# Query weights as one transfer and page loads re-divided between GpSimd and SyncE in a hybrid decoder step

## What is computed

```python
h  = adaLN(rmsnorm(x)) @ w_in                 # 512 query, 6 x 128 key/value, gates, 1536 delta-net columns, ...
kc = compress_rows(cached and new cmp rows)   # silu(blocks of 32 rows @ w1) @ w2
o  = g0 * attend(q, kc, vc) + g1 * attend(q, selected blocks) + g2 * attend(q, window)   # 8 heads, 2 key/value heads
d  = gated_delta_rule(conv(qkv))
x  = x + gate1 * (w_out @ [o | d])
x  = x + gate2 * mixture_of_experts(adaLN(rmsnorm(x)))
```

## Time and profile before

| what | us |
|---|---|
| median of 3 runs (1308.56 to 1320.38) | 1310.61 |
| the profiled execution | 1313.39 |
| its span, first to last instruction | 1311.3 |
| TensorE busy | 1024.7 (78%) |
| VectorE, ScalarE, GpSimd busy | 459.6, 270.5, 254.5 |
| projection and page loads, up to the next stage's first work | 0 to 299.2 |
| attention | 631.4 to 784 |

### The profile page before, as it was taken

One profiled execution on the slowest core, in us unless ns is written; L12 is line 12 of the kernel. 1 busy time (PEld: TensorE's weight loads), 2 busy tenths in 40 slices (PEclk: granted clock), 3 DMA queues, 4 the chain that ended last, 5 costly groups with the idle time before them and its releaser, 6 DMA issues. The chain is left out here.

```text
span 1311.3 us, 22398 instructions
## 1 busy us (share of the span) xinstructions
PE 1024.7 (78%) x8897; PEld 688.6 (53%) x8897; DVE 459.6 (35%) x889; ACT 270.5 (21%) x598; POOL 254.5 (19%) x413
## 2 busy tenths in 40 slices
PE   4999999686999598978699778793197877977850
PEld 1547677464567487976456443442055554544430
DVE  2200000025452355665478440436121222312217
ACT  4100000005531200112467330100011111111114
POOL 5000361301010445020356320000300000000014
PEclk9899999797988798988599988896599888988975
DMA  9973699828000200000643108404799899999944
GB/s 344 357 261 135 199 269 251 195 62 290 33 6 1 33 3 3 3 2 6 163 98 106 51 10 274 193 0 192 227 322 384 338 382 366 379 383 362 384 146 163
DMA packets 94869, 241.83 MB, mean 184 GB/s; under 512 B 30653, under 2 KB 53749, under 8 KB 79079
## 3 DMA queue, kind: packets, MB, share of 16 engines
q1 hardware_dynamic: 75610, 183.39, 39.9%
q0 software_dynamic: 12928, 46.55, 12.7%
q10 hardware_dynamic: 6228, 10.44, 2.5%
HBM read 254.83 MB, written 49.21 MB: 232 GB/s over the span
## 5 line engine op out<-in xcount | busy, mean ns | idle before, releaser
L2293 PE MATMUL PS<-ring,mixT 128*64 128x256 f32 x448 | 117.9, 423 | 40.7 <-DMA ring<-in_expert_w_down_dram 36.2
L2294 PE MATMUL PS<-ring,mixT 128*64 128x256 f32 (+2 forms) x656 | 131.7, 356 | 1.3 <-DVE mixT L2390 1.3
L2293 PEld LDWEIGHTS PS<-ring,mixT 128*64 128x64 f32 x448 | 67.3, 154 | 84.5 <-issue 60.9
L515 PE MATMUL PS<-hT,wring 128*128 128x288 f32 x256 | 84.9, 414 | 11.9 <-DMA wring<-in_w_in_dram 11.9
L2404 DVE COPY heT<-PS 128x128 f32<-128x128 f32 x49 | 14.3, 292 | 213.0 <-PE PS L2312 213.0
L2294 PEld LDWEIGHTS PS<-ring,mixT 128*64 128x64 f32 x656 | 81.2, 149 | 7.1 <-issue 6.8
L516 PE MATMUL PS<-hT,wring 128*128 128x288 f32 x256 | 84.1, 411 | 0.0
L2068 PE MATMUL PS<-ring,mixT 128*128 128x512 f32 (+1 forms) x160 | 74.4, 627 | 9.2 <-DMA ring<-in_w_out_dram 9.2
L2328 PE MATMUL PS<-ring,heT 128*64 128x512 f32 (+2 forms) x164 | 62.0, 499 | 3.6 <-DVE heT L2404 3.6
L515 PEld LDWEIGHTS PS<-hT,wring 128*128 128x128 f32 x256 | 48.9, 193 | 29.2 <-DMA wring<-in_w_in_dram 12.3
L2279 PE MATMUL PS<-ident,mixT 64*128 64x64 f32 x392 | 35.6, 233 | 32.6 <-DMA mixT<-xs_dram 32.6
(11 more groups left out here) (483 smaller groups left out, 2075.8 us busy)
## 6 DMA issues: line engine op xcount, KB each, us to landing
ring<-in_expert_w_gate_dram SPq DMA_DIRECT2D x40, 1024.0 KB
ring<-in_expert_w_up_dram SPq DMA_DIRECT2D x40, 1024.0 KB
ring<-in_expert_w_down_dram SPq DMA_DIRECT2D x40, 1024.0 KB
raw<-in_w_ada_dram SPq DMA_DIRECT2D x8, 2048.0 KB
xs_dram<-mixT POOLq DMA_DIRECT2D x49, 256.0 KB, 24.5
mixT<-xs_dram POOLq DMA_DIRECT2D x49, 256.0 KB
ys_dram<-yr ACTq DMA_DIRECT2D x98, 128.0 KB
slot<-in_expert_w_gate_dram SPq DMA_DIRECT2D x9, 1024.0 KB
```

The costliest lines, as they stand in the source:

```text
L515: MM(PS[:, b, 0:HALF], lhs, hT[:, k, 0:HALF], **s)
L2293: MM(PS[R, b, 0:DE], xT[:, n % 2, q, :], wg[:, q, :], **s)
L2294: last = MM(PS[Q, b, lo:hi], xT[:, n % 2, q, :], wu[:, q, lo:hi], **s)
```

## The change

Four edits. The query weights come as one transfer like the other groups, and TensorE picks the two heads' 64 columns itself: each unit now has, per k and half of the tokens, two products of 64 columns, one into output partitions 0 to 63 and one into 64 to 127. GpSimd takes over the second half of the cmp_v pages in the front stage. In the middle stage TensorE turns the first pages before it waits for the position tables, and VectorE writes positions after them, with a new semaphore `xp_ok`. In attention SyncE loads all selected keys and the values of samples 0 and 1; GpSimd loads the values of samples 2 to 7, four pages ahead of each of its units 2 to 7, and keys and values have semaphores of their own.

```diff
@@ stage_front
-        slot_dmas[g % 3].append(KD * KV if g == QG else 1)
+        slot_dmas[g % 3].append(1)
...
-                if g == QG:
-                    for k in range(KD):
-                        for v in range(KV):
-                            sp.dma_start(wring[:, g % 3, k, 0:512].rearrange("p (g v d) -> p g v d", v=KV, g=G)[:, :, v],
-                                         wv[:, k, v * G * HD:(v + 1) * G * HD].rearrange("p (g d) -> p g d", g=G)).then_inc(w_in[g % 3], 16)
-                else:
-                    sp.dma_start(wring[:, g % 3, :, 0:w], wv[:, :, c:c + w]).then_inc(w_in[g % 3], 16)
+                sp.dma_start(wring[:, g % 3, :, 0:w], wv[:, :, c:c + w]).then_inc(w_in[g % 3], 16)
...
-            load_pages(nc, sp, NB // 2, NB, m, t["cache_cmp_v"], raw[1], m.raw_in[1])
             sp.wait_ge(b_out, 64)
...
             load_pages(nc, pool, 0, NB, m, t["cache_cmp_k"], raw[0], m.raw_in[0])
+            pool.wait_ge(b_ps, KD)
+            load_pages(nc, pool, NB // 2, NB, m, t["cache_cmp_v"], raw[1], m.raw_in[2])
...
-                    if chan:
+                    if g == QG:
+                        for hf in range(2):
+                            for v in range(KV):
+                                last = MM(PS[v * HD:(v + 1) * HD, b + hf, 0:HALF], wring[:, g % 3, k, (v * G + i) * HD:(v * G + i + 1) * HD],
+                                          hT[:, k, hf * HALF:(hf + 1) * HALF], **s)
+                    elif chan:
@@ stage_middle
+            def positions(s):
+                for v in range(KV):
+
+                    last = V.tensor_copy(xT[:, v, :, HCOL:], posT[:, s, :].rearrange("p (h r) -> p r h", r=OCT))
+                last.then_inc(xp_ok, 1)
...
+            take_pages(0)
             dve.wait_ge(pos_ps, 1)
             V.tensor_copy(posT[:, :, :], PS[:, 4, 0:2 * LP].rearrange("p (s l) -> p s l", s=2)).then_inc(pos_ok, 1)
             dve.wait_ge(pos_ok, 1)
-            take_pages(0)
+            positions(0)
...
+            turn_pages(0)
             pe.wait_ge(p_in, 16 * 2)
...
             last.then_inc(pos_ps, 1)
-            turn_pages(0)
...
             pe.wait_ge(tr_a, NU)
+            pe.wait_ge(xp_ok, 1)
@@ stage_attention
+    FIRST_LOAD = 2
...
+            def selected_keys(a):
+                load_pages(nc, sp, 2 * a, 2 * a + 2, m, t["cache_sel_k"], m.pages[:, SEL_K], selk_in[a])
...
-            selected(0)
+            selected_keys(0)
...
+            selected_keys(1)
             sp.dma_start(m.V[:, 1], window("cache_win_v")).then_inc(winv_in, 16)
...
-            for a in range(1, NB // 2):
-                selected(a)
+            load_pages(nc, sp, 0, 2, m, t["cache_sel_v"], m.V[:, 0], selv_in[0])
+            selected_keys(2)
+            selected_keys(3)
...
                 kind, br, a, g = units[u]
+                if FIRST_LOAD <= u < FIRST_LOAD + NB - 2:
+                    load_pages(nc, pool, u - FIRST_LOAD + 2, u - FIRST_LOAD + 3, m, t["cache_sel_v"], m.V[:, 0], selv_in[1])
...
-                        pe.wait_ge(*((sel_in[units[u][2]], 16 * 4 * PAGES) if br == SEL else (wink_in, 16)))
+                        pe.wait_ge(*((selk_in[units[u][2]], 16 * 2 * PAGES) if br == SEL else (wink_in, 16)))
...
                     if br == SEL and a == 0:
                         pe.wait_ge(new_in, 32)
+                        pe.wait_ge(selv_in[0], 16 * 2 * PAGES)
+                        pe.wait_ge(selv_in[1], 16 * (NB - 2) * PAGES)
```

More of the change, by code:

```diff
@@ L572, in stage_middle @@
     w_in, p_in, w2_in = [sem(f"c_w_in{s}") for s in range(2)], sem("c_p_in"), sem("c_w2_in")
+    xp_ok = sem("xp_ok")
     pos_ps, pos_ok, tr_ps, tr_a, tr_v = sem("pos_ps"), sem("pos_ok"), sem("tr_ps"), sem("tr_a"), sem("tr_v")
@@ L751, in taps @@
                         ins.then_inc(conv_ok, 1)
+            def positions(s):
+                for v in range(KV):
+                    last = V.tensor_copy(xT[:, v, :, HCOL:], posT[:, s, :].rearrange("p (h r) -> p r h", r=OCT))
+                last.then_inc(xp_ok, 1)
             def take_pages(s):
-                for v in range(KV):
-                    V.tensor_copy(xT[:, v, :, HCOL:], posT[:, s, :].rearrange("p (h r) -> p r h", r=OCT))
                 for n in range(NU):
@@ L772, in _ @@
             dve.wait_ge(hid_ps, KV * NHC)
+            positions(1)
             take_pages(1)
@@ L807, in turn_pages @@
                     if n == 1:
-                        pe.wait_ge(m.raw_in[s], 16 * NB * PAGES)
+                        pe.wait_ge(m.raw_in[s], 16 * (NB if s == 0 else NB // 2) * PAGES)
+                    if s == 1 and n == 1 + NB // 2:
+                        pe.wait_ge(m.raw_in[2], 16 * NB // 2 * PAGES)
                     for j in range(4):
@@ L889, in _ @@
             pe.wait_ge(tr_a, 2 * NU)
+            pe.wait_ge(xp_ok, 2)
             pe.wait_ge(w_in[1], 16)
@@ L1520, in stage_attention @@
     strip_in = [sem(f"a_strip_in{k}") for k in range(5)]
-    sel_in, wink_in, winv_in, new_in, bias_in = [sem(f"a_sel_in{a}") for a in range(NB // 2)], sem("a_wink_in"), sem("a_winv_in"), sem("a_new_in"), sem("a_bias_in")
+    selk_in, selv_in, wink_in, winv_in, new_in, bias_in = [sem(f"a_selk_in{a}") for a in range(NB // 2)], [sem(f"a_selv_in{k}") for k in range(2)], sem("a_wink_in"), sem("a_winv_in"), sem("a_new_in"), sem("a_bias_in")
     gate_out, gate_in, sg, qs_ok = sem("a_gate_out"), sem("a_gate_in"), sem("a_sg"), sem("a_qs_ok")
@@ L1600, in _ @@
                 sp.dma_start(strip[:, :, lo:hi], bass.AP(m.rb_rep, RB_C - (SEQ - P) + lo, [[H * RB_W - 1, P], [RB_W, H], [1, hi - lo]])).then_inc(strip_in[k], 16)
-            def selected(a):
-                load_pages(nc, sp, 2 * a, 2 * a + 2, m, t["cache_sel_k"], m.pages[:, SEL_K], sel_in[a])
-                load_pages(nc, sp, 2 * a, 2 * a + 2, m, t["cache_sel_v"], m.V[:, 0], sel_in[a])
+            def selected_keys(a):
+                load_pages(nc, sp, 2 * a, 2 * a + 2, m, t["cache_sel_k"], m.pages[:, SEL_K], selk_in[a])
             window = lambda name: t[name][0].rearrange("b (g p) k d -> p (b g) (k d)", p=P)
@@ L2532, in build @@
         m.rows_out = nc.alloc_semaphore("rows_out")
-        m.raw_in = [nc.alloc_semaphore(f"raw_in{s}") for s in range(2)]
+        m.raw_in = [nc.alloc_semaphore(f"raw_in{s}") for s in range(3)]
         m.ident = sb("ident", [P, P])
```

## The result

The changed kernel takes 1319.05 us (median of 20 runs, 1312.65 to 1325.78) where the kernel before takes 1310.78 beside it (20 runs). The ratio is 1.0062, interval 1.0043 to 1.0082: 8 us slower, within the 1% that was forecast, and not 1 us faster as the forecast's sum had it.

The account below looks back on a forecast made before the run. TensorE, busy 78%, was held by three 11 to 13 us waits: query weights, position tables (hiding a late barrier), samples' pages. Front -11.0, attention +23.5 and -13.7 sum to -1.2 us: forecast 1311, range 1298 to 1328.

Parts of the forecast that it names:

- Query group: End of the first stage: weights land in time, products take 31 us, TensorE ends at about 275.8 instead of 289.7.
- halves one after the other: Rival in the query group: paired 64-column products run serially, TensorE ends at 306.8, total 1328 us; chance 4%.
- GpSimd's last page: First stage: GpSimd, now with 48 pages, issues its last at 289.8, including 1 us delay from larger query weight transfers.
- Plus 1.4 for the barrier = 291.2.: First stage's end: only a 1.4 us barrier follows GpSimd's last page, so the middle stage starts turning pages at 291.2.
- The front and middle: First and middle stages together: 11.0 us saved, bounds -14 to -6.
- GpSimd ends no earlier than SyncE did: Rival in the front: slow page price for all 48 pages, last out at 303, front +2, total 1325; chance 6%.
- Attention, the cost: Units 2 to 7: GpSimd's four-page batches delay gate products, about 5.5 us a unit; +23.5 us, bounds +18 to +30.
- Attention, the gain: Samples' part of attention: TensorE's page waits and the half clock after them go; -13.7 us, bounds -12 and -15.
- The rule on VectorE and GpSimd's transfers: Attention: busy VectorE locks GpSimd out while writing descriptors; 24 loads could cost up to 60 us.
- The rival of dear pages: Attention: every GpSimd page costs 2.2 us, a batch 9.1 instead of 5.5, +21.6, total 1333; chance 12%.
- GpSimd hides its pages.: Rival in attention: loads fall into GpSimd's idle time, total 1288, half hidden 1300; chance 12% for 1300 or below.
- The sum: Whole kernel: -11.0 + 23.5 - 13.7 = -1.2 us, forecast time 1311.

Follow-up runs that it names:

- e7: Changed kernel with the query weights' last group in sixteen strided transfers and full-width products again; ratio 1.0051 to the kernel before (+6.7 us).
- e2: Changed kernel with attention's loads as before: SyncE loads keys and values of each pair, GpSimd none; ratio 0.9985 to the kernel before (-2.0 us).
- e3: Changed kernel with GpSimd's 24 attention value pages given to SyncE, keys still ahead of values; ratio 0.9871 to the kernel before (-16.9 us).
- e9: Changed kernel with GpSimd's 24 attention pages loaded one ahead of each of units 2 to 25, without the loop; ratio 0.9918 to the kernel before (-10.7 us).
- e5: Changed kernel with GpSimd also waiting for its last pages' arrival before the first stage ends; ratio 1.0069 to the kernel before (+9.0 us).
- e10: Changed kernel with the staging buffers' zero fills in 18 transfers instead of 66, same bytes; ratio 1.0047 to the kernel before (+6.2 us).

## Why the prediction came out as it did

The time was forecast as 1311 and is 1319; "within 1%" and the range hold, the sign of the sum (-1.2) does not. The attention part came out as worked out. The front part did not: 9 of its 11 us never came, and that the time still lies within 1% is the width of the band, not the merit of that part. By its steps:

**Query group.** Right. TensorE had the weights in time, took 31.26 us for the 128 products (256 passes) and ended at 275.7 (275.8). The rival of halves one after the other is out.

**SyncE's pages.** Right: its 16 pages take 21.99 and are out at 260.7 (265).

**GpSimd's last page.** Right: 289.85 (289.8). The 1 us for larger weight transfers among the zeros fits e7, where the last page is out 1.4 earlier, but is not shown by it: in six profiles with the same first stage the drain begins between 289.2 and 290.9.

**"Plus 1.4 for the barrier = 291.2."** This term failed. It was read from SyncE's end to the next stage, where the barrier is all that is left. Behind GpSimd's last page a drain of 9.62 and 1.1 of barrier follow. The kernel before had the drain of 8.52 in the same place, with nothing behind it; the change took its cover away. The first page turn came at 300.73 and not at 291.2, beyond the 297 that had been named as a sign of being wrong. The front and middle gave 2.0 by e2's time and 0.1 to 0.9 by the profiles (end of the middle stage 427.1 in the changed kernel and 426.3 in e2, 427.2 before) instead of 11.0, below the bound of 6: no bound had been set on GpSimd's way to the barrier. The 0.6 for the position copies can't be told from how much the middle stage varies between profiles. The rival "GpSimd ends no earlier than SyncE did" named this outcome with the wrong cause: the page price was the fast one, 1.28.

**Attention, the cost.** Right: +23.5 forecast, 25.0 measured by e3. A batch took 5.57 (5.5), six from unit 1 to 7 took 34.2 (33.0), units 8 to 10 gave 1.6 back (1.3). For the low clock behind the stretch 3 was forecast: from unit 10 to unit 27 the changed kernel takes 44.3 us and e3 41.4, with the clock at 0.50 up to 680 and 0.81 from 680 to 690, so 2.9. The drain at attention's end is longer by 2.0 for 24 more transfers. Its row, in the kernel before and in the changed one:

```profile
L1570 POOLq DRAIN  x1: 1154/1154/1154, 776.9 to 776.9; - x1
```

```profile
L1581 POOLq DRAIN  x1: 3147/3147/3147, 783.8 to 783.8; - x1
```

It costs nothing here. It is over at 786.9, and two other engines still have work then; their own DRAIN rows in the changed kernel begin only when that is done:

```profile
L1581 DVEq DRAIN  x1: 1217/1217/1217, 788.8 to 788.8; - x1
...
L1581 ACTq DRAIN  x1: 452/452/452, 790.4 to 790.4; - x1
```

**Attention, the gain.** Right: 13.7 forecast, 14.9 by the times of e2 and e3, 14.0 by their profiles. Net +10.1 (+9.8), and the stage itself shows the same. Its barriers, at the end of the delta stage and at its own end, in the kernel before and in the changed one:

```profile
L932 POOLq EVENT_SEMAPHORE  x2: 17/17/17, 630.5 to 630.5; - x2
L1570 POOLq EVENT_SEMAPHORE  x2: 17/17/17, 784.0 to 784.1; - x2
```

```profile
L942 POOLq EVENT_SEMAPHORE  x2: 17/17/17, 627.2 to 627.3; - x2
L1581 POOLq EVENT_SEMAPHORE  x2: 17/17/17, 790.9 to 791.0; - x2
```

That is 153.6 us before and 163.7 now.

**The rule on VectorE and GpSimd's transfers.** No sign of it: GpSimd's page issues in attention take 0.54 to 0.61, and its pages follow at 1.17 each, faster than the 1.28 of the front. In the changed kernel that tests little, since VectorE is busy only 1.8 to 2.9 of each 10 us there. In e9 it is busy about 7.6 of 10 from 650 to 680, and an issue takes 0.58 to 0.61 all the same. The rule of the Trainium skill ("SBUF — State Buffer", section "SBUF: two separate sides"), by which an issue could take five times as long, has its 3100 ns from a VectorE copy; beside these issues VectorE ran reductions, reciprocals, work that reads PSUM and a few subtractions within SBUF, and what a copy within SBUF would do no run here shows. The rival of dear pages is out.

**"GpSimd hides its pages."** Out for the batches, and right for the same pages one at a time. I had argued that a batch of 5.4 does not fit into an idle 1.0. That holds for the batch; a single page, 0.6 beside a product, does fit.

**The sum.** -2.0 + 25.0 - 14.9 = +8.1. The difference to -1.2 is 9.0 of lost front, 1.5 of cost and -1.2 of gain; only the first of the three is larger than the times can tell apart.

## What to carry to other kernels

Before an engine's work is moved past the point that ends a stage, look up what the engine still does between its last issue and the barrier; on GpSimd that is a drain that grows with the transfers issued, and it is free only while another engine is later (at the end of the first stage it no longer was, at the end of attention it still is). Work put on a half idle engine should be cut so that each piece fits into the idle time between two items of that engine's own chain: in the attention stage the same 24 loads cost 24 us four at a time in a row and less than 1 us one at a time. And an edit whose gain is covered by another engine, as the query weights here (nothing in the changed kernel, 10 us at the start of the next stage with the pages on SyncE), has to be judged again once that engine is out of the way.

## What the runs showed of the hardware

GpSimd drains for 5.9 to 9.6 us at the end of the first stage, about 0.08 us for every transfer that it issued in it, whether the data has landed (e5) or not, with the bytes unchanged (e10), and 0.083 each in attention, though the last of those 24 was issued over 100 us earlier.

That is the price of plain transfers, not of every DRAIN row. The row begins while GpSimd still has work in hand and counts that too: in the delta stage of the kernel before it takes 4.1 us from 571.2 with no transfer issued, while GpSimd's last product runs until 575.2. And the ten indirect transfers (addresses from a table in SBUF) with which the route stage ends are dearer. In the changed kernel, last issue and drain:

```profile
938.61 0.89 POOL L2069 DMA_INDIRECT xs_dram<-h,pos  x1 [0.30 <-issue]
```

```profile
L1999 POOLq DRAIN  x1: 12591/12591/12591, 931.2 to 931.2; - x1
```

The drain ends at 943.8, 4.3 us behind the last issue, 0.4 for each of the ten. All other engines are done by 928.7, so this one is paid in full, before the change (12.67 us from 924.5) as after it.

Attention's pages show that GpSimd's load of a page number runs beside its own elementwise product (e9), but not beside its transfer issues in a row. Products of 64 columns into two halves of the array, one token stream for both, run as pairs: 64 pairs (two passes each) in 31.26 us, 0.49 a pair, what one product over all 128 columns took before.
